# A hybrid decoder layer on one core: small loads moved to ScalarE's queue, latent squares folded on VectorE, splits moved, first passes reordered

## The reference

```python
h = rmsnorm(x, g_pre_mix) * (1 + scale_m) + shift_m
z = h @ w_in
(q_lat, kv_lat, k_rope, gq, gk, gv, g_lr, g_og, gate_a, gate_b) = jnp.split(z, IN_OFFSETS, axis=-1)
y_a = mla_branch(q_lat, kv_lat, k_rope, positions, ...) @ w_branch_a     # rmsnorm(q_lat), rmsnorm(kv_lat), 8 heads
y_b = gla_branch(gq, gk, gv, g_lr, g_og, ...) @ w_branch_b               # gated linear attention, 4 heads
y = (sigmoid(gate_a) * y_a + sigmoid(gate_b) * y_b) @ w_mix_out
x = x + gate_m * rmsnorm(y, g_post_mix)
h = rmsnorm(x, g_pre_ffn) * (1 + scale_f) + shift_f                      # "h2" in the kernel
f = conv_ffn(h, w_ffn_up, conv_w, conv_b, w_ffn_down)
return x + gate_f * rmsnorm(f, g_post_ffn)
```

## Time and profile before

| | |
|---|---|
| median of 3 runs | 1621.44 us (1621.06 to 1622.4) |
| profiled execution | 1620.52 us |
| its span | 1618.7 us |
| PE busy | 1578.9 us, 98% |
| DVE busy | 1135.8 us, 70% |
| ACT busy | 818.3 us, 51% |
| moved by DMA | 389.33 MB, mean 241 GB/s |

### The profile page before, as it was taken

How to read it: one execution, slowest core, us unless ns; L and a number is a source line. 1 busy time by engine, 2 the same in 40 slices (tenths; PEclk the granted TensorE clock), 3 DMA queues, 4 the chain that set the end, 5 groups by cost and what they waited for, 6 DMA issues and landing times.

```text
span 1618.7 us, 29394 instructions
## 1 busy us (share of the span) xinstructions
PE 1578.9 (98%) x11709; PEld 1485.1 (92%) x11709; DVE 1135.8 (70%) x1323; ACT 818.3 (51%) x1064; POOL 7.3 (0%) x11
## 2 busy tenths in 40 slices
PE   3999999999999999999999999999999999999998
PEld 3999999879999999999888999999999999888886
DVE  6778877887877696877756677777777665644444
ACT  4557776656544643444446554555545454434332
POOL 0000000001000000000000000000000000000000
PEclk9999999999999999999999999999999999999999
DMA  9999988874459897877864677777777666555553
GB/s 331 318 327 348 314 286 236 299 247 158 131 183 303 276 295 245 287 268 266 324 235 131 216 239 236 245 238 252 236 234 231 192 197 208 182 190 198 184 194 143
DMA packets 197150, 389.33 MB, mean 241 GB/s; under 512 B 18487, under 2 KB 31545, under 8 KB 196297
## 3 DMA queue, kind: packets, MB, share of 16 engines
q1 hardware_dynamic: 192457, 371.38, 68.6%
q10 hardware_dynamic: 4610, 16.79, 3.1%
HBM read 386.02 MB, written 2.10 MB: 240 GB/s over the span
## 4 chain that ended last, share of the span: by engine, by line
PE 93%; DVE 4%; ACT 2%; DMA 1%; issue 1%; SPq 0%; DVEq 0%; ACTq 0%
PE ps L570 20%; PE ps L572 20%; PE ps L574 20%; PE ps L597 8%; PE ps L599 8%; PE ps L598 8%; PE ps L755 2%; DVE w_lo L1326 1%; DMA ada_first<-in_w_ada 1%; ACT w_hi L925 1%; PE ps L694 1%; PE ps L662 0%; PE ps L545 0%; PE ps L770 0%; PE ps L693 0%
## 5 line engine op out<-in xcount | busy, mean ns | idle before, releaser
L1326 DVE TENSOR_TENSOR w_lo<-raw,w_hi 128x1024 fp32r<-128x1024 f32 x530 | 625.3, 1221 | 432.3 <-ACT w_hi L925 431.5
L925 ACT ACTIVATE w_hi<-raw 128x1024 fp32r<-128x1024 f32 x530 | 532.8, 1052 | 658.2 <-PE ps L574 433.4
L570 PE MATMUL ps<-h2t,w_hi 128*128 128x256 f32 x1408 | 390.1, 277 | 2.2 <-DVE w_lo L1326 1.6
L572 PE MATMUL ps<-h2t,w_hi 128*128 128x256 f32 x1408 | 388.8, 276 | 0.0
L574 PE MATMUL ps<-h2t,w_lo 128*128 128x256 f32 x1408 | 388.8, 276 | 0.0
L570 PE MATMUL ps<-ht,w_hi 128*128 128x256 f32 x1136 | 318.4, 280 | 0.0
L572 PE MATMUL ps<-ht,w_hi 128*128 128x256 f32 x1136 | 314.7, 277 | 0.0
L574 PE MATMUL ps<-ht,w_lo 128*128 128x256 f32 x1136 | 314.7, 277 | 0.0
L570 PEld LDWEIGHTS ps<-h2t,w_hi 128*128 128x128 f32 x1408 | 264.4, 188 | 2.6 <-DVE w_lo L1326 1.8
L572 PEld LDWEIGHTS ps<-h2t,w_hi 128*128 128x128 f32 x1408 | 264.4, 188 | 0.0
L574 PEld LDWEIGHTS ps<-h2t,w_lo 128*128 128x128 f32 x1408 | 264.3, 188 | 0.0
(11 more groups left out here) (274 smaller groups left out, 1999.4 us busy)
## 6 DMA issues: line engine op xcount, KB each, us to landing
raw<-in_w_ffn_up SPq DMA_DIRECT2D x176, 512.0 KB, 4.5
raw<-in_w_in SPq DMA_DIRECT2D x168, 512.0 KB, 5.2
ada<-in_w_ada SPq DMA_DIRECT2D x148, 512.0 KB, 6.7
raw<-in_w_ffn_down SPq DMA_DIRECT2D x88, 512.0 KB, 4.2
raw<-in_w_branch_b SPq DMA_DIRECT2D x32, 512.0 KB, 5.4
raw<-in_w_mix_out SPq DMA_DIRECT2D x32, 512.0 KB, 5.0
ada<-in_w_ada ACTq DMA_DIRECT2D x32, 512.0 KB, 4.1
raw<-in_w_branch_a SPq DMA_DIRECT2D x16, 512.0 KB, 5.6
```

The costliest lines, as they stand in the source:

```text
L570: mm(o, w_hi[:, s, k, cols], moving[:, kt, 0], start=opens, stop=False, skip_group_check=True)
L572: mm(o, w_hi[:, s, k, cols], moving[:, kt, 1], start=False, stop=False, skip_group_check=True)
L925: A(w_hi[:, slot], raw[:, slot], ACT.Copy).then_inc(hi_done, 1)
L1326: V.tensor_tensor(w_lo[:, slot], raw[:, slot], w_hi[:, slot].bitcast(F32), ALU.subtract)\
```

## The change

1. The transfers of constants, positions, c, b_ada and g_pre_mix leave SP's queue and are issued by ACT, in this order, before its first table load. SP begins with x.
2. `busy(5)` runs for `ada_used` 12 to 15 instead of 10 to 15.
3. In the passes over the first k tiles, the order misc, qlat, gq0, gq1, gk0 becomes gq0, gq1, gk0, qlat, misc. The later passes keep theirs.
4. In step LAT+1, behind its two splits, DVE adds the squares: tile 1 to tile 0, tiles 4 and 5 to tiles 2 and 3, then tile 3 to tile 2. PE waits for the three additions and multiplies two tiles by ones instead of six.
5. The splits of units u0+4 and u0+5 move from behind h2 to between its groups: on ACT behind b=4, on DVE behind b=5.

```diff
-PASSES = ([(kind, g, 0, 2) for kind, g in FIRST + SECOND] + [(kind, g, 4, 2) for kind, g in FIRST + SECOND]
+PASSES = ([(kind, g, 0, 2) for kind, g in FIRST[2:] + FIRST[1::-1] + SECOND] + [(kind, g, 4, 2) for kind, g in FIRST + SECOND]
...
-            for dst0, v in ((96, c[0]), (0, b_ada[0]), (112, g_pre_mix[0])):
-                n = v.shape[0] // P
-                small(rows[dst0:dst0 + n, 0, :], as_rows(v), first_rows_loaded)
-            sp.dma_start(fixed[:], const_f).then_inc(const_loaded, 16)
-            sp.dma_start(pos_i[:], positions[0:1, :].to_broadcast([P, S])).then_inc(pos_loaded, 16)
...
-                pe.wait_ge(lat_squared, 1)
+                pe.wait_ge(lat_folded, 3)
                 pe.wait_ge(mod_ready, 8)
-                for n, (f0, nf) in enumerate(((0, 2), (2, 4))):
-                    for i in range(nf):
-                        ins = mm(ps[:, 4, n * S:(n + 1) * S], ones[:], lat_sq[:, f0 + i, :], start=i == 0,
-                                 stop=i == nf - 1)
+                for n, f0 in enumerate((0, 2)):
+                    ins = mm(ps[:, 4, n * S:(n + 1) * S], ones[:], lat_sq[:, f0, :], start=True, stop=True)
...
-            for a in range(10, 16):
+            for a in range(12, 16):
...
+            nc.scalar.dma_start(fixed[:], const_f).then_inc(const_loaded, 16)
+            nc.scalar.dma_start(pos_i[:], positions[0:1, :].to_broadcast([P, S])).then_inc(pos_loaded, 16)
+            for dst0, v in ((96, c[0]), (0, b_ada[0]), (112, g_pre_mix[0])):
+                n = v.shape[0] // P
+                nc.scalar.dma_start(rows[dst0:dst0 + n, 0, :], v.rearrange("(r c) -> r c", c=P))\
+                    .then_inc(first_rows_loaded, 16)
             nc.scalar.preload_act_table(ACT.Silu)
...
+                if b == 4:
+                    for j in (2, 3):
+                        split_at(u0, j, t0, p0)
...
-            for j in range(2, 6):
+            for j in (4, 5):
                 split_at(u0, j, t0, p0)
...
+            def lat_fold():
+
+                dve.wait_ge(lat_squared, 1)
+                V.tensor_tensor(lat_sq[:, 0], lat_sq[:, 0], lat_sq[:, 1], ALU.add).then_inc(lat_folded, 1)
+                V.tensor_tensor(lat_sq[:, 2:4], lat_sq[:, 2:4], lat_sq[:, 4:6], ALU.add).then_inc(lat_folded, 1)
+                dve.wait_ge(lat_folded, 2)
+                V.tensor_tensor(lat_sq[:, 2], lat_sq[:, 2], lat_sq[:, 3], ALU.add).then_inc(lat_folded, 1)
...
                 if k == LAT + 1:
                     dve.wait_ge(vec_ready, 1)
+                    lat_fold()
                     lat_scale(0)
...
+                if b == 5:
+                    split(2 * FFN + 4, (2 * FFN + 4) % RING)
+                    split(2 * FFN + 5, (2 * FFN + 5) % RING)
...
-            for j in range(2, 6):
+            for j in (4, 5):
                 split_at(u0, j)
```

More of the change, by code:

```diff
@@ L310, in build @@
         recip_x, attn_zero, suffix_ready = sem("recip_x"), sem("attn_zero"), sem("suffix_ready")
-        pre_ready, og_folded = sem("pre_ready"), sem("og_folded")
+        pre_ready, og_folded, lat_folded = sem("pre_ready"), sem("og_folded"), sem("lat_folded")
         h_ready, h_hi, h_lo = sem("h_ready"), sem("h_hi"), sem("h_lo")
@@ L1187, in _ @@
             name, value = PAIRS[FFN - 1][2]
-            u0 = 2 * FFN
+            u0, (t0, p0), a0 = 2 * FFN, START[PAIRS[FFN][0]], 5 * ADA_BLOCK
             split(u0 + 2, (u0 + 2) % RING, total[u0 + 2], SEM[name], value)
@@ L1198, in _ @@
             act.wait_ge(recip_1, 1)
-            for c in range(3):
-                cols = slice(c * UC, (c + 1) * UC)
+            for q in range(3):
+                cols = slice(q * UC, (q + 1) * UC)
                 A(xn1[:, 1, cols], x1[:, 1, cols], ACT.Copy, scale=stat[:, 7:8]).then_inc(norm_1, 1)
@@ L1219, in _ @@
             nc.scalar.preload_act_table(ACT.Gelu_apprx_tanh)
-            u0, (t0, p0), a0 = 2 * FFN, START[PAIRS[FFN][0]], 5 * ADA_BLOCK
-            for j in range(2, 6):
+            for j in (4, 5):
                 split_at(u0, j, t0, p0)
```

## The result

The changed kernel takes 1630.4 us (median of 5 runs, 1629.6 to 1631.67) against 1621.44 (1621.06 to 1624.08): a ratio of 1.0053, interval 1.0038 to 1.0067. It is slower, by some 9 us in this comparison. The forecast was +1.0 us, with a range up to 1625.4. It isn't the quotient of the two medians, and where the times scatter most the two differ by up to 1.5 us.

The account below looks back on a forecast made before the run. PE was taken as the bound, ending last for 93% of the span. Start -4.4, fold +4.6, clock +2.4 and splits -1.6 made +1.0 us on 1621.44: 1622.4, 8 in 10 from 1617.6 to 1625.4.

Parts of the forecast that it names:

- Start: Kernel start: small loads on ACT's queue, x first, fewer dummies; first adaLN columns at 34.0 instead of 38.46, -4.4 us.
- (b): Kernel start: end of the angle work, which needs positions and c_act; angles end at 11.9, c_act there at 7.7.
- landings of 1.7 and 4.1 us: Kernel start: times to landing taken for the last small load, issued at about 2.6; there at 4.3 or 6.7.
- The bound of 13.9 for T: Kernel start: upper bound of T, allowing 2 us more for pos_i under load, for which no row existed.
- T: Start of VectorE's adaLN chain, the later of first piece's landing and (b); taken as 12.4, bounds 11.9 to 13.9.
- this sign of being wrong: Kernel start: the prediction is wrong if VectorE's first adaLN piece starts after 14 us.
- The rival: Kernel start: small loads come late beside x; +3.3 us, 1624.7, or 1626.2 at 11 us; chance 0.16.
- The fold: Latent squares' sums: additions queue behind VectorE's splits, PE idles about 6.2 us; +4.6 us, plus +2.4 for the clock's fall.
- The FFN entry: Third FFN pair: splits moved into h2 remove PE's stall for a low part; -1.6 us (-1.4 to -1.8).
- The 1.56 us in brackets: Third FFN pair: PE's stall until 896.50 for the low part of units 4 and 5, in the kernel before.
- The margin of the fourth pair: Fourth FFN pair: delayed last groups of h2 and splits end at about 899.3, before PE wants them at 900.7.
- Dummies and order: Kernel start: dropping 10 dummies, 2.3 us, frees PE before the 16th adaLN piece; new order of first passes, zero.

Follow-up runs that it names:

- `fold_fill`: Fold of the squares behind the splits, alone on the kernel before, plus 26 dummy matmuls ahead of PE's wait: 1628.94 against 1624.65 us, 1.0023.
- `hold_x`: Changed kernel with SP holding x until the five small loads have landed: 1627.42 us against 1624.65 of the kernel before, 1.0017.

## Why the prediction was wrong

**Start: wrong, and it carries the miss.** Forecast -4.4 us, measured +1.0 us between the two traces, and +3.8 us for the loads alone. The step that failed is (b), the time at which c_act is there. I took it to be there by 7.7 us at the latest, with the last small load landing at 4.3 to 6.7, from landings of 1.7 and 4.1 us; it landed at 11.4, and c_act was there at 12.45. The first row is of a load with hardly more than small loads beside it, the second of one half-megabyte stream beside another in the middle of the kernel. Neither had a queue of ten megabytes for company. The bound of 13.9 for T, "2 us more", was a guess with no row, and T was 17.56. The prediction had named this sign of being wrong, a first piece after 14 us. The rest of the start went by the steps: VectorE ended 21.6 us after T (17.56 to 39.17), the columns followed at 39.23, the weights were no longer late (their high part started at 34.41).

The rival had this mechanism and its direction, with too small a price (+3.3 us in all) and too small a chance. With T=17.56 in place of 12.4 the prediction's own sum gives 17.56+21.5+0.1=39.16 against 38.46, so +0.7 for the start and +6.1 in all, which is near the 6.2 measured, in part by luck: the start is too good by more than 1 us against the other traces, and the fold too dear by 1.5. The sentence of the Trainium skill beside it, that transfers of different engines run on the same 16 DMA engines and interleave (DMA: Bandwidth & Descriptors, section Issuing engines are not separate DMA queues), agrees with the trace, but what matters here is the price of interleaving: four times the time to landing for 8 KB, 8.2 us against 2.1.

**The fold: right in mechanism and sign, the clock's part too large.** Forecast +7.0 us (4.6 of stall, 2.4 of clock), measured +5.5 (+5.0 by the ratio, interval 3.2 to 6.8). The wait was 6.0 to 6.3 us as forecast, and the clock fell. The stall was 4.4 us where PE was kept busy (`fold_fill`), close to the 4.6. With the fold alone the next pair came 5.2 us later against the pair ahead of the sums, and the delay was 6.3 us when the clock was back: 1.9 us of clock, not 2.4. Then some of it came back, 0.8 us in that trace (5.6 from 291 on). In the changed kernel the delay was 9.1 us at 262 and 8.3 from 291 on. Until 268 of the trace before, 132 matmuls follow one another every 0.113 us in the changed kernel and every 0.118 us in the one before, which makes 0.6 us, and PE waits 0.2 us less for w_lo behind them.

The sentence of the Trainium skill (TensorE: Matmul & The Clock Gate, section What's actually happening), that the throttled level is the default and activity releases it, agrees with the four traces in which nothing filled a wait of 6 us: the clock fell in each.

**The FFN entry: right.** -1.6 forecast, -2.3 between the traces, -1.8 by the times. The 1.56 us in brackets count from the modelled end of the last matmul. From start to start there are 1.84 us (894.66 to 896.50) where matmuls otherwise follow every 0.12 us, so the stall cost 1.7 us. Two pairs take 13.14 us in the kernel before and 11.41 with the splits alone, again 1.7 us less. In the changed kernel they take 11.00, because its matmuls follow one another more closely here; why isn't shown. The margin of the fourth pair held.

**Dummies and order.** 1.7 us of the start's gain was to come from the dummies; alone the fewer dummies brought 0.5 us by the medians and 1.3 by the ratio (interval -2.8 to +0.3). The 1.7 us were those of one execution; in other traces the dummies held the columns up by 0.2 to 1.6 us. In the changed kernel VectorE was so late that they had no say. The order was zero, as forecast.

**The base.** I took 1621.44 as the median of the kernel before; three sets of 30 or 31 runs put it at 1624.1 to 1624.7. Against these the forecast of +1.0 missed by 5 us, not by 8. A scatter of 7 us, in large part of clock falls of 1.5 to 3 us each, should have been in the range. Taken singly the parts add up: 2.5 us of start (from the traces), 5.5 of the fold and -1.8 of the splits make 6.2.

## What to carry to other kernels

A small load on a second queue isn't ahead of a big one on the first: the small loads that gate the start must land before the stream begins, and here a wait of 4 us on SP for them cost nothing. An operation given from PE to another engine waits for all that this engine has queued before it; ask first what those instructions wait for, since here it was PE itself. And a kernel's time is to be known from many executions before an edit of a few microseconds is judged by it.

## What the runs showed of the hardware

A load of 8 KB lands in 2.1 to 2.4 us beside other small loads alone (`hold_x`), and in 8.2 to 8.9 us beside x and the adaLN pieces issued on another queue; 128 KB take 3.0 us and 9.2 to 9.6 us. SP's x, 1 MB at a time, lands in 6.0 us instead of 7.3 to 7.6 when it starts after them.

The clock falls not only after idle time, and not each time after the same work. In the changed kernel PE was counted as busy from 405.04 to 409.0 with matmuls of one column each, and stood at the lower level from 408.4 to 415.0, 3.0 us lost:

```profile
405.04 3.96 PE L649 MATMUL ps<-ones,acc 128*128 128x1 f32 x32
```

Sixteen of the same form, 1.95 us behind a wait of 0.75, stand right ahead of the fall near 227. In the trace of the kernel before the 32 run from 396.77, and the clock stays at 1.00 until 411.

At a granted clock of 1.00 the distance between the main matmuls of 256 columns is 0.113 us in some stretches and 0.118 us in others, in the same kernel; nothing here shows why.
